# Half products in the first stage, the first head's inputs beside the dt product, pieces and quarters in the last head, and a new order in the scan's first chunk

## What is computed

```python
u = rms_norm(hid, norm_pre_w)
proj = einsum('bsd,de->bse', u, w_in)          # 6672 columns: q k v g z x b c dt
attn = mixture_of_dilations(q, k, v)           # 16 heads of 64; patterns (128,1) (512,4) (2048,16)
attn = attn * silu(g_attn)
xs, b_mat, c_mat = split(silu(causal_depthwise_conv(xbc)))
dt = softplus(dt_raw + dt_bias)
y = ssd_chunked(xs, dt, -exp(a_log), b_mat, c_mat) + d_skip * xs    # 16 heads, chunks of 128
y = gated_group_rms_norm(y, z, ssm_norm_w)
return hid + rms_norm(concat(attn, y) @ w_out, norm_post_w)
```

## Time and profile before

| | |
|---|---|
| median of three runs | 2393.36 us |
| the profiled execution | 2392.45 us |
| its span | 2390.7 us |
| TensorE busy (matmuls) | 2274.2 us, 95% |
| VectorE busy | 1052.4 us, 44% |
| ScalarE busy | 826.7 us, 35% |
| GpSimd busy | 711.5 us, 30% |
| mean granted TensorE clock | 0.979 |

### The profile page before, as it was taken

One profiled execution on the slowest core, in us unless ns is written; L12 is line 12 of the kernel. 1 busy time (PEld: TensorE's weight loads), 2 busy tenths in 40 slices (PEclk: granted clock), 3 DMA queues, 4 the chain that ended last, 5 costly groups with the idle time before them and its releaser, 6 DMA issues. The chain is left out here.

```text
span 2390.7 us, 34105 instructions
## 1 busy us (share of the span) xinstructions
PE 2274.2 (95%) x12565; PEld 1948.9 (82%) x12565; DVE 1052.4 (44%) x2245; ACT 826.7 (35%) x2013; POOL 711.5 (30%) x348
## 2 busy tenths in 40 slices
PE   6899999999999999999994999999998599999998
PEld 4788888888888888888884999999998478888886
DVE  4200000001111122456556777777777856666661
ACT  5311111111111111112124777777776322222221
POOL 0011011101011010011112456556652445555552
PEclk9999999999999999999997999999999699999999
DMA  4322122122322121212226555565655434444431
GB/s 133 97 79 75 57 79 88 27 79 60 90 79 79 36 79 53 80 53 79 71 90 128 128 143 142 135 150 118 141 135 193 172 110 137 135 136 137 137 106 53
DMA packets 243225, 244.82 MB, mean 102 GB/s; under 512 B 76836, under 2 KB 218336, under 8 KB 231424
## 3 DMA queue, kind: packets, MB, share of 16 engines
q1 hardware_dynamic: 241984, 235.55, 35.2%
q0 software_dynamic: 1104, 7.47, 0.8%
HBM read 160.67 MB, written 73.66 MB: 98 GB/s over the span
## 5 line engine op out<-in xcount | busy, mean ns | idle before, releaser
L442 PE MATMUL mm<-u_hi,w_hi 128*128 128x512 f32 x1696 | 666.1, 393 | 16.2 <-DVE u_lo L371 14.2
L443 PE MATMUL mm<-u_lo,w_hi 128*128 128x512 f32 x1696 | 662.7, 391 | 0.0
L444 PE MATMUL mm<-u_hi,w_lo 128*128 128x512 f32 x1696 | 662.5, 391 | 0.0
L254 POOL TENSOR_TENSOR w_lo<-w_raw,w_hi 128x1024 fp32r<-128x1024 f32 x53 | 139.5, 2633 | 1090.1 <-ACT w_hi L268 1090.1
L442 PEld LDWEIGHTS mm<-u_hi,w_hi 128*128 128x128 f32 x1696 | 320.1, 189 | 84.0 <-DVE u_lo L371 17.3
L444 PEld LDWEIGHTS mm<-u_hi,w_lo 128*128 128x128 f32 x1696 | 320.0, 189 | 67.0
L443 PEld LDWEIGHTS mm<-u_lo,w_hi 128*128 128x128 f32 x1696 | 320.2, 189 | 65.8
L417 DVE COPY tok_tile<-turn 128x512 f32<-128x512 f32 x104 | 64.6, 684 | 578.6 <-PE turn L457 576.5
L1213 PE MATMUL ps_t<-ident_b,probs 128*128 128x128 f32 x1136 | 214.3, 278 | 13.8 <-DVE probs_t L1063 7.9
L1700 PE MATMUL ps_out<-wo_hi,mix_hi 128*128 128x512 f32 x512 | 208.1, 406 | 1.3 <-ACT mix_hi L1651 1.3
L1701 PE MATMUL ps_out<-wo_lo,mix_hi 128*128 128x512 f32 x512 | 200.7, 392 | 0.0
(11 more groups left out here) (189 smaller groups left out, 3492.9 us busy)
## 6 DMA issues: line engine op xcount, KB each, us to landing
feat<-fm SPq DMA_DIRECT2D x28, 1024.0 KB, 4.7
w_raw<-in_w_in_dram SPq DMA_DIRECT2D x52, 512.0 KB, 6.1
tok<-tok_tile SPq DMA_DIRECT2D x26, 1024.0 KB, 5.6
raw_q<-feat SPq DMA_DIRECT2D x32, 512.0 KB, 6.2
raw_k<-feat SPq DMA_DIRECT2D x32, 512.0 KB, 6.5
cum_b<-cum_scratch SPq DMA_DIRECT2D x16, 1024.0 KB, 7.6
cls_nat<-cls_out SPq DMA_DIRECT2D x64, 132.0 KB, 2.7
tok_tile<-in_x_dram SPq DMA_DIRECT2D x16, 512.0 KB, 3.6
```

The source lines that it names most:

```text
L254: pool.tensor_tensor(w_lo[b][:, :, :], w_raw[b][:, :, :], w_hi[b][:, :, :].bitcast(F32), ALU.subtract).then_inc(w_lo_made[b], 1)
L442: pe.matmul(mm[tb][:, :], w_hi[b][:, k, :], u_hi[:, k, block_cols(tb)], start=(k == 0), stop=False)
L443: pe.matmul(mm[tb][:, :], w_hi[b][:, k, :], u_lo[:, k, block_cols(tb)], start=False, stop=False)
L444: last = pe.matmul(mm[tb][:, :], w_lo[b][:, k, :], u_hi[:, k, block_cols(tb)], start=False, stop=(k == KT - 1))
```

## The change

- **First stage.** `EARLY` becomes `HALVES`: each of the six products between the tiles is cut in two parts of 12 matmuls, one behind each of the tiles 4 to 15. The first product of a token block now stands one tile later than before, behind the transposes of the next block's first tile. ScalarE's reads of them (`EARLY_READ`) move to tiles 6, 8, 10, 12, 14 and behind the loop, ahead of `u_hi`.
- **First head.** All of SBUF gets fixed addresses (`place`, `Rooms`), so that the first head's tiles (`FirstHead`) can be filled while `project` still runs. GpSimd's identity and near mask move to the program's start, the seven mask steps to VectorE behind the first stage. In the last pair SyncE loads raw k, and raw q once the last feature product is done (`load_first_head`); ScalarE takes the high parts of q ahead of the last tanh and those of k behind it; GpSimd splits q, VectorE splits k and sorts q, all beside the dt product. The wait for the dt store moves from the end of `project` to SyncE's start in `attend`.
- **Last head.** The decay of chunk 0 becomes 16 instructions of 128 columns in 8 pieces of two, at steps 9, 11, 13, 15, 21, 23, 25 and 27 of head 15, with the small exponents at step 7. The merge of head 15 goes in quarters: GpSimd multiplies one half of it (`part_b`), VectorE the other and adds, and TensorE turns each quarter once it is merged.
- **Scan, chunk 0.** VectorE does `diag_and_gate(0)`, `small_exponents(1)` and `segments(1)` ahead of the first `take_low`; 12 tiles of `take_low` follow `mix_low(0)`. ScalarE takes 12 tiles' high parts at once at the start. TensorE turns chunk 0 behind `read_state(1)`.

```diff
-        EARLY = {3: (0, 0), 5: (1, 0), 7: (0, 1), 9: (1, 1), 11: (0, 2), 13: (1, 2)}
+        HALVES = {4 * (tb + 1) + 2 * b + half: (b, tb, half)
+                  for tb in range(TB - 1) for b in range(2) for half in range(2)}
+
+        EARLY_READ = {i + 2: (b, tb) for i, (b, tb, half) in HALVES.items() if half == 0 and i + 2 < TT}
...
-                    if i in EARLY:
-                        b, tb = EARLY[i]
-                        pe.wait_ge(u_lo_made, 2 * (tb + 1) * TB)
-                        multiply(0, b, tb)
+                    if i in HALVES:
+                        b, tb, half = HALVES[i]
+                        if b == 0 and half == 0:
+                            pe.wait_ge(u_lo_made, 2 * (tb + 1) * TB)
+                        multiply(0, b, tb, range(half * KT // 2, (half + 1) * KT // 2))
...
+                def load_first_head():
+
+                    sp.wait_ge(fm_out[0], 16 * (before_pair(STORED, "k", D_ATTN // (2 * P)) + 1))
+                    for x, at in (("k", D_ATTN), ("q", 0)):
+                        if x == "q":
+                            sp.wait_ge(product[TB - 1], FT)
+                        for rows in (slice(0, HEAD_DIM), slice(HEAD_DIM, P)):
+                            sp.dma_start(first.raw[x][rows, :], dram["feat"][at:at + HEAD_DIM, :])\
+                              .then_inc(first.raw_in[x], 16)
...
+                        if is_last(pair) and b == 1:
+                            take_high("q")
...
+                take_high("k")
...
+                dve.wait_ge(first.high_made["k"], TB)
+                dve.wait_ge(fm_made[1], PAIRS)
+                dve.tensor_tensor(first.k_rest[:, :], first.raw["k"][:, :], first.k_high[:, :].bitcast(F32), ALU.subtract)\
+                   .then_inc(first.split["k"], 1)
+                dve.wait_ge(first.split["q"], 1)
+                dve.wait_ge(fm_out[1], 16 * total_pairs(STORED))
...
-                load_qk(0)
...
+        SEG_STEPS = (9, 11, 13, 15, 21, 23, 25, 27)
...
+                def first_small():
+
+                    dve.wait_ge(S["cum_in"], 16)
...
+                    for h in heads:
+                        done = dve.tensor_scalar(early.seg[:, h, :], early.cum_b[:, h, :], cum_tok[:, 0, h:h + 1], 0.0,
+                                                 ALU.subtract, ALU.min)
...
+                    if pair == HEADS // 2 - 1 and b == 1:
+                        if s == SEG_STEPS[0] - 2:
+                            first_small()
...
-                merge(dve, HEADS - 1, 1)
-                for n in range(4):
-                    gate_read(n, HEADS // 2 - 1, last_banks[n])
+                for n in range(TB):
+                    dve.tensor_tensor(part_a[:, quarter(n), :], nat_out[1][:, quarter(n), :],
+                                      scale[:, 0, quarter(n)].unsqueeze(2).broadcast_to([P, TT // TB, HEAD_DIM]), ALU.mult)\
+                       .then_inc(last_part, 1)
+                    dve.wait_ge(last_part, n + 1)
+                    dve.wait_ge(last_cls, n + 1)
+                    dve.tensor_tensor(merged[:, quarter(n), 1, :], part_a[:, quarter(n), :], part_b[:, quarter(n), :], ALU.add)\
+                       .then_inc(last_merged, 1)
+                    if n >= 1:
+                        gate_read(n - 1, HEADS // 2 - 1, last_banks[n - 1])
+                gate_read(TB - 1, HEADS // 2 - 1, last_banks[TB - 1])
...
-                take_low(PORTION[0])
                 for c in range(CHUNKS):
                     diag_and_gate(c)
                     if c < LAST:
                         small_exponents(c + 1)
                         segments(c + 1)
+                    if c == 0:
+                        take_low(PORTION[0])
                     if c >= 2:
                         out_scale(c - 2)
-                    if c == 0:
-                        take_low(PORTION[1])
                     if c < LAST:
                         weigh(c + 1)
                         off_and_skip(c + 1)
                     mix_low(c)
                     if c == 0:
+                        take_low(PORTION[1])
                         take_low(PORTION[2])
                         take_low(PORTION[3])
...
-                take_high(PORTION[0])
+                for i in range(3):
+                    take_high(PORTION[i])
...
-                    turn(c)
+                        turn(c)
                     if c < LAST:
                         mix_b_and_c(c + 1)
                         read_state(c + 1)
+                    if c == 0:
+                        turn(c)
```

More of the change, by code:

```diff
@@ L49, with place, __init__, __call__ @@
 CONVOLVED = "xbc"
+KB = 1024
+def place(nc, name, at, shape, dt=F32):
+    with ExitStack() as ctx:
+        if at:
+            ctx.enter_context(nc.sbuf_tensor(f"under_{name}", [P, at // 4], F32))
+        return ctx.enter_context(nc.sbuf_tensor(name, shape, dt))
+class Rooms:
+    def __init__(self, nc, start, end):
+        self.nc, self.at, self.end = nc, start, end
+    def __call__(self, name, shape, dt=F32):
+        room = place(self.nc, name, self.at, shape, dt)
+        self.at += -(-4 * math.prod(shape[1:]) // 32) * 32
+        assert self.at <= self.end, (name, self.at, self.end)
+        return room
+U_END = 128 * KB
+W1_AT = 150 * KB
+W_LO1_AT = 158 * KB
+FM1_AT = 162 * KB
+CONV_AT = 170 * KB
+TANH_AT = CONV_AT + 8 * KB + 32
+TOK_AT = TANH_AT + 8 * KB
+SPARE_AT = TOK_AT + 8 * KB
+RAW_K_END = SPARE_AT + 8 * KB
+MASKS_AT = RAW_K_END + KB
+TINY_AT = MASKS_AT + 4 * KB
+SBUF_END = TINY_AT + 768
+class FirstHead:
+    def __init__(self, nc, ctx):
+        self.raw = {"q": place(nc, "raw_q", W1_AT, [P, SEQ]), "k": place(nc, "raw_k", SPARE_AT, [P, SEQ])}
+        self.q_parts = place(nc, "q_parts0", TOK_AT, [P, SEQ], F32R)
+        self.q_class = place(nc, "q_class0", FM1_AT, [P, CLASSES, SEQ // CLASSES], F32R)
+        self.k_high = place(nc, "k_high0", CONV_AT, [P, SEQ], F32R)
+        self.k_rest = place(nc, "k_rest0", TANH_AT, [P, SEQ], F32R)
+        spare = Rooms(nc, MASKS_AT, TINY_AT)
+        self.ident = spare("ident_b", [P, P])
+        self.near_mask = spare("near_mask", [P, 2, CLASSES, P // CLASSES])
+        self.class_mask = spare("class_mask", [P, SEQ // CLASSES])
+        def sem(name):
+            return ctx.enter_context(nc.semaphore(name))
+        self.made = sem("made")
+        self.masks_made = sem("masks_made")
+        self.raw_in = {x: sem(f"{x}_in") for x in "qk"}
+        self.high_made = {x: sem(f"{x}_high_made") for x in "qk"}
+        self.split = {x: sem(f"{x}_split") for x in "qk"}
+        self.q_sorted = sem("q_sorted")
+        self.dt_out = sem("dt_out")
 def before_pair(kinds, kind, pair):
@@ L445, in multiply @@
                                          start=False, stop=(k == KT - 1))
-                    last.then_inc(product[tb], 1)
+                    if part[-1] == KT - 1:
+                        last.then_inc(product[tb], 1)
                 def turn_tile(kind, pair, b):
@@ L542, in __init__, with attend @@
         self.wo_in = [ctx.enter_context(nc.semaphore(f"c_wo_in{t}")) for t in range(KO)]
-        with nc.sbuf_tensor("wo_raw", [P, KO, D_MODEL], F32) as self.wo_raw, \
-             nc.sbuf_tensor("seg", [P, SSM_HEADS, CHUNK], F32) as self.seg:
-            pass
-def attend(nc, dram, dt_bias, a_log, early, w_out, d_skip, ssm_norm_w):
+        self.wo_raw = [place(nc, f"wo_raw{t}", at, [P, D_MODEL]) for t, at in enumerate(WO_AT)]
+        self.seg = place(nc, "seg", EARLY_END, [P, SSM_HEADS, CHUNK])
+def attend(nc, dram, dt_bias, a_log, first, early, w_out, d_skip, ssm_norm_w):
     with ExitStack() as ctx:
-        def sb(name, shape, dt=F32):
-            return ctx.enter_context(nc.sbuf_tensor(name, shape, dt))
         def sem(name):
@@ L933, in _ @@
                 head_turn(HEADS - 1, 1, has_next=False)
+                pool.wait_ge(scales_made, HEADS)
+                for n in range(TB):
+                    pool.tensor_tensor(part_b[:, quarter(n), :], cls_nat[1][:, :, n, 0:HEAD_DIM],
+                                       scale[:, 1, quarter(n)].unsqueeze(2).broadcast_to([P, TT // TB, HEAD_DIM]), ALU.mult)\
+                        .then_inc(last_cls, 1)
                 pool.wait_ge(stored, 16 * (HEADS // 2))
```

279 lines of the change are left out of this document (153 added, 126 removed).

## The result

The changed kernel takes 2369.5 us (median, 2369.12 to 2372.19), the kernel before 2392.35 (2391.11 to 2394.46): a ratio of 0.9906, 95% interval 0.9889 to 0.9923. That is faster, as forecast, but by 22.9 us where 32.9 were summed up, and 1.5 us above the range. The profiled execution has a span of 2367.7 us against 2390.7, so 23.0 us are to be explained. All times of this document leave out three executions that took over 4000 us, one of the first experiment and two of the kernel before.

What follows compares the result with a forecast made beforehand. TensorE, busy 95% of the span, was taken as the bound, so only its waits and low clock could give time. Gains 17.5 + 11.2 + 0.2 + 4.0 = 32.9 us off 2392.45 gave 2359.6, 2360 for the median; range 2352 to 2368.

Steps and rivals of the forecast that it cites:

- Part A: First stage: the new order leaves no TensorE wait but the first low-clock stretch; gain 17.5 us, bounds 14 and 18.5.
- Rival 1: First stage: transposes mixed with matmuls keep the clock at the lower level, 26 us more, 2386 us; chance 0.04.
- Part B: First head: preparing q and k beside the dt product shortens TensorE's 23.31 us wait; gain 11.2 us.
- rival 2: First head: v arrives late, about 1280, so the gain is 5.1 in place of 11.2, 2366 us; chance 0.10.
- Part C: Last head: losses and gains nearly cancel; gain 0.2 us, bounds a loss of 4 and a gain of 4.
- TensorE loses 2.7: Last head, step 7: VectorE stands still 3.6 us with the small steps, 1 us covered; bounds 0 and 3.6.
- the quarters: Behind the last head: merging in quarters overlaps VectorE, GpSimd, TensorE and reads; gain 1.2 us, bounds -1 to 2.
- The small steps: Last head: 16 small decay instructions on VectorE, perhaps 0.2 us each, cost 0.4 us; bounds 0 and 2.
- the decay out of the tail: Behind the last head: with the decay moved earlier, merge_drops can start sooner; gain 2.1 us.
- Part D: Scan, chunk 0: VectorE's 4.74 us wait goes, a 1 us wait comes; gain 4.0 us, bounds 1 and 6.5.
- VectorE does the same work in another order: Scan, chunk 0: VectorE's work is unchanged, only reordered, so its 4.74 us wait ahead of the second weights goes.
- Rival 5: Projection: fixed addresses slow its 5088 matmuls; at 10 ns each 51 us, 2411 us; chance 0.03.

Runs made afterwards that it cites:

- the first experiment: Changed kernel with first_small at step 12 of the last head in place of 7, decay pieces moved behind it: 2362.5 us, ratio to before 0.9878.

## Why the prediction was wrong

**Part A** was right, and undersized by 1.65 us. Its check holds: no idle time over 0.7 us, and the last block's first product starts at 70.86 (72.4 forecast). The low clock at the start lasted for 6 matmuls or so, not 12: from 29.48 on they start 0.23 us apart. A tile then took 3.63 us, and the first product started 0.5 us later than before. Rival 1 did not occur: 8 transposes between every 12 matmuls did not bring the clock down, the granted clock was 1.00 from 30 us on. The Trainium skill, TensorE: Matmul & The Clock Gate, "PE-mode transpose", says that a transpose doesn't count as busy in the same way; in these rows it did no harm, and no run here tests transposes without matmuls beside them.

**Part B** was right. The first probabilities came 12.35 us behind the last matmul of the dt product, 24.85 before: 12.5 against 11.2. The logarithm and the table load behind it stand where they were forecast, and nothing else comes between. Rows of ScalarE in the changed kernel, to lay beside the earlier trace rows:

```profile
1249.67 0.42 ACT L1273 ACTIVATE part_b<-part_a 128x256 f32<-128x256 f32 x1
1250.10 1.28 ACT L1283 ACT_TABLE_LOAD   x1
1251.40 0.40 ACT L1283 ACTIVATE probs<-masked,cls_out 128x128 f32<-128x128 f32 x1
```

The stretch from the end of the dt product's last matmul (0.39 us behind its start, from which the table counts) to head 1 varies by executions: 55.8 to 59.7 us in twelve with the new order (mean 57.1), 67.5 to 69.9 in five with the old (mean 69.1). So B is worth 12.0 us. v was on time, rival 2 did not occur.

**Part C** is the first step that failed, with 5.35 of the 10 us. That `first_small` waits for `cum_b` was forecast, and its size on VectorE (3.10 us measured, 3.3 forecast) too. Mis-sized was the term "TensorE loses 2.7": it lost 7.2. It had two holes. The first is the copy, which took 1.62 us and not 0.17: it was held to the end of GpSimd's addition for head 14's merge, and TensorE waited 4.20 us. Without these 1.45 us the wait would have been 2.75, as forecast. The kernel before already had that addition at the time of the forecast landing, 1821.5, but the prediction looked at GpSimd only for the quarters:

```profile
1820.67 2.38 POOL L770 TENSOR_TENSOR merged<-part_a,part_b 128x1024 f32<-128x1024 f32 x1
```

The second hole is the clock, which went to its lower level behind the wait and cost 3.0 us more; the sum had no term for it. Rows for this were in the first stage of the kernel before, and part A was built on them: the waits of 3.15 and 4.43 us were followed by matmuls at twice the spacing. But the prediction read too much into them where it says that this came "after each wait". Behind the wait of 2.17 us at 89.97 the matmuls start 0.23 us apart from the second on:

```profile
90.31 0.39 PE L443 MATMUL mm<-u_lo,w_hi 128*128 128x512 f32 x1
90.54 0.39 PE L444 MATMUL mm<-u_hi,w_lo 128*128 128x512 f32 x1
```

And behind one of 1.78 us in head 15 they ran at the lower level for 6.8 us. So the length of a wait doesn't tell it by itself.

The small steps cost 0.36 (0.4 forecast), the decay out of the tail gave 2.07 (2.1), and the quarters 0.33 (1.2). The last was missed for the contention with GpSimd, which the prediction had named for its lower bound: multiplying and adding a quarter took 0.89 and 0.72 us beside it, 0.41 and 0.42 alone. The Trainium skill, SBUF — State Buffer, "Who interferes with whom", has a VectorE instruction with two SBUF inputs contend with a GpSimd instruction that reads SBUF; here the trace agrees (0.89 us against 0.41).

**Part D** is the second, with 3.8 us. The mechanism was right as far as it went: the 4.74 us wait is gone, and the new wait of 1 us for the exponentiated decay didn't come either. The step that failed is "VectorE does the same work in another order" with the same durations. VectorE's list from the first `cb` to the second `new_state` took 51.73 us, 51.95 before: what it no longer waits, it needs for three groups beside GpSimd, 8.03 + 4.62 in place of 4.62 + 6.34, 5.69 in place of 3.99, and 2.81 in place of 1.23, 5.0 us in all, less 0.4 for the gating. The forecast counted on less contact with GpSimd; the new order put more of VectorE's work, the two-input subtractions, beside it.

**The third loss, 4.9 us behind `turn(1)`, had no term.** 3.6 of it are 14 chunks at 0.26 us, the distance of w_out's low parts. Rival 5 named fixed addresses as the one thing that could slow matmuls, but it looked at the projection of the first stage, where the spacing stayed at 0.227 us, and gave it 0.03. In the scan it was true, at 3 to 5 ns for each matmul on and behind a tile that is off. The prediction did name a steady chunk over 30.15 us as a sign of being wrong, but no term of its sum had it. The other 1.3 us are at the first of these chunks, where the stretch from `turn(1)` to the projection's second half took 5.25 us at a granted clock of 0.50, in place of 4.34 at 0.61; this stretch varies by executions, and the chunk with it: 30.1 to 31.7 us in the runs made from the kernel before, 30.5 to 32.0 in those made from the changed one. So what of the 1.3 us belongs to the change is open.

The sum: 1.65 + 2.55 - 5.35 - 3.8 - 4.9 = -9.9 us, the miss.

## What to carry to other kernels

A wait that TensorE gets costs its length, and it can cost the matmuls at the lower clock behind it: here 4.2 us became 7.2, and 1.8 became 5.1. Add both outcomes to the range. Work that is moved is no longer beside the same neighbour: list what GpSimd does in the new place, and take the durations measured beside it, for the shortest copy too. And a change of the memory's layout is a change of the inner loop: keep operands that TensorE reads in turn at the distance that they had, or, as was free here, a multiple of 256 bytes from it.

## What the runs showed of the hardware that was not expected

- Two moving operands were read in turn by 64 matmuls of 512 columns in a chunk. Where 7 or 16 of the 16 tiles of one lay 32 or 64 bytes off a multiple of 256 from the other, the chunk took 0.23 to 0.29 us more; 256 bytes off, or both moved by 64, cost at most 0.04.
- A VectorE copy of 128x16 elements beside a GpSimd addition of 128x1024 ended 0.02 to 0.03 us behind that addition in six kernels, and took 1.18 to 2.00 us; begun before the addition it took 0.18.
- A VectorE min with one SBUF input (128x2048) took 2.81 us while GpSimd multiplied, 1.23 alone; four subtractions of 128x1024 took 8.03 and 4.62.
- A TensorE wait of 1.78 us in the last head was followed by 6.8 us at a granted clock of 0.50; one of 2.17 us in the first stage was not.
